# A mixture-of-experts kernel: seven blocks that hold the last halves of two experts each, with their own weight slots

## The chip, the cores and the metric

The kernel runs on one core of a Trainium2 chip. The metric is the device time in microseconds of one execution, lower is better. The core has five engines that run side by side and wait for each other by semaphores: TensorE (PE; its weight loads are listed as PEld), VectorE (DVE), ScalarE (ACT), GpSimd (POOL) and SyncE (SP), the last used for issuing transfers alone. Transfers run on 16 DMA engines that all queues share.

## What is computed

One layer of a streaming encoder for 4096 prompt rows and 128 sample rows of width 1024, 4224 tokens in all, everything in float32. First a Mamba-2 group and a gated spatial MLP on one input projection, an output projection and a residual; then a mixture of experts, and a last norm. The change is in the mixture:

```
h2 = rms_norm(x, norm2_g)
group  = argmax of 4 group logits;  p_group = its softmax
top 2 of the 8 experts of that group;  weights = p_group * softmax(top 2)
for each (token, expert) pair, sorted by expert, padded to blocks of 128:
    y = (silu(xb @ w_gate[e]) * (xb @ w_up[e])) @ w_down[e]      # 1024 -> 256 -> 1024
out[token] += weight * y
x = x + out;   y_out = rms_norm(x, final_norm_g)
```

There are 32 experts and 2 x 4224 = 8448 pairs. An expert's weights take 3.15 MB: 2.10 MB for gate and up, 1.05 MB for down. For the inputs of the reference the router gives the experts 161 to 445 pairs each.

## The kernel before

Two phases. **Phase 1** walks the 33 tiles of 128 tokens: projections, convolution, scan, output projection, norm and router. Each tile stores its rows x2 (after the residual) and h2 (normed) to HBM, and scatters, for each pair, the token number and its weight into a list per expert (`slot_d`). **Phase 2** is the mixture.

Between them VectorE makes tables (`dve_tables`, L1374 to L1434) from the counts: each expert's count is rounded up to blocks of 128, and for each block of the schedule the tables say where its list stands (`row_i`), in which of the weight slots its expert is, how many weight loads must have landed, and, for each load, which expert and after which block. GpSimd gathers the lists with one indirect transfer (L1480), TensorE turns them (L1597), VectorE writes the index rows: `tok_i` (which row to gather), `first_i` and `last_i`. Each token has two pairs in different blocks. The block that holds the earlier one stores its weighted result to `first_d`; the later one gathers it back, adds it to its own and to x2, takes the norm and stores y. An index that is out of bounds makes the transfer skip that row, so each block does both, each for a part of its rows. In the same stretch VectorE and TensorE update the sample streams' states (L1079, L1080, L553).

Phase 2 runs blocks in pairs (`over_pairs`, L1361): at least 33 pairs, more behind a branch. The blocks go by a software pipeline. For block b the engines do this:

- **TensorE** (`pe_phase2`): gate and up of block b + 1 (L1581, 8 calls that give 16 instructions of 128x512), transposes of block b's gated rows (L1614), transposes of block b + 2's gathered rows (L1566), down of block b (L1621, 4 calls, 8 instructions).
- **ScalarE**: evicts the transposes (L1651, L1640), silu of block b + 1 (L1646), squares of block b - 1 for the norm (L1662), half of the down result times its weight (L1659).
- **VectorE**, in this order: adds the earlier result to block b - 1 (`add_first`, L1684), gate of block b + 1 (L1680), half of the rows of block b + 2 (`rows1`, L1674), the other half of the down result (L1699), the norm of b - 1 (L1688), the residual of b (L1707).
- **GpSimd** (`step`, L1521), all on one queue in this order: gather of the rows of block b + 4 (L1500), the root for b - 1 (L1515), store to `first_d` (L1528), gather of x2 for b + 1 (`residual`, L1529), store of y for b - 1 (L1532), and, after the store to `first_d` has landed, the gather of the earlier results for b + 1 (`earlier`, L1533). Its transfers are listed at the helpers' lines L1488 and L1493.
- **SyncE** (`sp_phase2`) loads the experts in order into four weight slots, two transfers each (L1225, L1228). Three experts are loaded ahead (`load_first`); the k-th load waits until the blocks of expert k - 4 have done their gate matmuls, its down part until they have done theirs.

The tail behind the last block is one addition, square, root, norm and store (L1720 to L1722, L1544 to L1558). SyncE ends the kernel when `all_stored` comes.

Of the kernel before, what the change touches and what calls it, by code (L numbers as in the profile page):

```python
# [21 lines left out]
P = 128  # L22
# [52 lines left out]
NCONST = C_ONES + NE  # L75
# [40 lines left out]
GB = 4  # L116
AHEAD = 4
WSLOTS = 4
SET = 3


def build(nc, x_rows, x_cols, consts_in, cols_in, bcast_in, w_in, w_out, w_out_T_in, ws_in, ws_smp_in, cache_in, st_old_in,
          st_T_in, slot_in, w_exp, final_g, y_out, conv_prompt, ssm_prompt, conv_sample, ssm_sample, gmlp_v_sample):
    ctx = ExitStack()
    with ctx:
# [16 lines left out]
        first_d = nc.dram_tensor("first_rows", [T, D], F32).ap()  # L142
# [21 lines left out]
        ones = cst[:, C_ONES:NCONST]  # L164
# [65 lines left out]
        spare = sb("spare", [P, 4])  # L230
# [5 lines left out]
        row_i = sb("row_i", [P, 1], I32)  # L236
# [43 lines left out]
        const_loaded, cols_loaded, bc_loaded, ws_loaded = (sem(n) for n in ("const_loaded", "cols_loaded", "bc_loaded", "ws_loaded"))  # L280
# [11 lines left out]
        gf_loaded = sem("gf_loaded")  # L292
        dve_step, pool_step = sem("dve_step"), sem("pool_step")

        x2_tiles, h2_tiles, first_tiles = (d.rearrange("(t p) d -> t p d", p=P) for d in (x2_d, h2_d, first_d))
# [32 lines left out]
        m_buf = [take(D), xT_mem[1][:, 0:D]]  # L328
        xr_buf = [xT_mem[0][:, 0:D], g2_b]
# [234 lines left out]
        def pe_phase1(pe):  # L564
# [11 lines left out]
            pe.wait_ge(const_loaded, 16)  # L576
# [505 lines left out]
        def dve_phase1(dve):  # L1082
# [38 lines left out]
            dve.wait_ge(ws_loaded, 16)  # L1121
            dve.wait_ge(const_loaded, 16)
# [120 lines left out]
        def sp_turn(sp, tn):  # L1243
# [17 lines left out]
            if tn.prev:  # L1261
                sp.wait_ge(s["x2_part"], 3 * i)
                sp.dma_start(at_tile(x2_tiles, i - 1), x_res[v][:, :]).then_inc(x2_stored, 16)
                if tn.end:
                    load_first(sp, 2)
                sp.wait_ge(s["h2_ready"], i)
                sp.dma_start(at_tile(h2_tiles, i - 1), h2[:, :]).then_inc(h2_stored, 16)
# [30 lines left out]
        def sp_phase1(sp):  # L1298
# [25 lines left out]
            sp.dma_start(flat(wsT[:, :, :]), ws_in).then_inc(ws_loaded, 16)  # L1324
# [49 lines left out]
        def dve_tables(dve, st):  # L1374


            nb, some, pend, pstart, nth = (eqt[:, :], em[:, :], oh[:, 0, :], oh[:, 1, :], oh[:, 2, :])
            ni = slots32[:, 0:NE]
            col = [rt[:, c:c + 1] for c in range(12)]
            block, ebase, kth, start, place, last = col[0:6]  # L1380
            dve.wait_ge(s["rank_read"], NT)
            st.link(V.tensor_tensor(ni, carry[:, :], to_count, ALU.add))
            st.link(V.tensor_scalar(ni, ni, 7, None, ALU.logical_shift_right))
            st.link(V.tensor_copy(nb, ni))
            st.inc(V.tensor_scalar(some, nb, 1.0, None, ALU.min))
            st.link(V.tensor_tensor_scan(out=pend, data0=ones[:, 0:NE], data1=nb, initial=0.0, op0=ALU.mult, op1=ALU.add))

            cmp = rk[:, :]
            st.link(V.tensor_scalar(cmp, pend, tok0, None, ALU.is_le))
            st.inc(V.tensor_reduce(ebase, cmp, AX.X, ALU.add))  # L1390
            st.inc(V.tensor_tensor(pstart, pend, nb, ALU.subtract))
            st.link(V.memset(some[:, 0:SET], 1.0))
# [3 lines left out]
            oe = lgs[:, 0:NE]  # L1396
            st.link(V.tensor_scalar(oe, iota_e, ebase, None, ALU.is_equal))
            st.link(V.tensor_tensor(oe, oe, pstart, ALU.mult))
            st.link(V.tensor_reduce(start, oe, AX.X, ALU.add))
            st.link(V.tensor_tensor(place, tok0, start, ALU.subtract))  # L1400
            st.link(V.tensor_scalar(place, place, float(T // P), float(NE * T // P), ALU.min, ALU.add))
            V.scalar_tensor_tensor(out=row_i[:, :], in0=ebase, scalar=float(T // P), in1=place, op0=ALU.mult,
                                   op1=ALU.add).then_inc(s["rows_ready"], 1)
            dve_h2(dve, NP, NP % 2)

            st.inc(V.tensor_tensor_scan(out=nth, data0=ones[:, 0:NE], data1=some, initial=0.0, op0=ALU.mult, op1=ALU.add))
# [4 lines left out]
            st.inc(V.tensor_scalar(tcol[:, 1:2], kth, 1.0, None, ALU.add))  # L1411
            st.link(V.tensor_copy(ni[:, 0:1], kth))
            st.link(V.tensor_scalar(ni[:, 0:1], ni[:, 0:1], WSLOTS - 1, None, ALU.bitwise_and))
            st.link(V.tensor_scalar(ni[:, 1:2], ni[:, 0:1], 1, None, ALU.logical_shift_right))
# [437 lines left out]
```

## Time and profile before

| | us |
|---|---|
| median of 3 runs | 2912.54 (2911.41 to 2916.14) |
| the profiled execution | 2912.39 |
| its span | 2910.5 |
| TensorE busy | 2859.1 |
| VectorE busy | 1580.8 |
| ScalarE busy | 806.9 |
| GpSimd busy | 878.5 |

Phase 1 takes the first two thirds of the span, the tables some 25 us from 1951, phase 2 from 1976 to the end. Busy time counts an engine's instructions, not its waits and not what its sequencer does. A row of a timeline is the start, the duration, engine, line, operation, out<-in with shapes, the number of merged instructions, and in brackets the idle time ahead with what ended it. In the list of transfers the last number is the median time from issue to landing.

### The profile page before, as it was taken

To read this page: it belongs to the slowest core of one execution; us is meant where nothing else is said; L and a number is where in the kernel's file an instruction comes from. 1 tells how busy PE (TensorE), PEld (TensorE's weight loads), DVE (VectorE), ACT (ScalarE), POOL (GpSimd) and SP (SyncE) were. 2 spreads that over 40 slices of the span, in tenths; PEclk is the share of its full clock that TensorE was granted. 3 is DMA by queue.
4 is the path that set the end of the run, shared out by engine and by line. 5 is a ranking of instruction groups with operands and counts; after the bars stand their busy time and mean duration, and the time that the engine had idled before them with its cause. 6 is when DMAs were issued, how large, how long until landed. Compare 5 with 4: busy or idle time off the path is not lost.

```text
span 2910.5 us, 38335 instructions
## 1 busy us (share of the span) xinstructions
PE 2859.1 (98%) x12809; PEld 1890.8 (65%) x12809; DVE 1580.8 (54%) x4163; ACT 806.9 (28%) x1517; POOL 878.5 (30%) x1366
## 2 busy tenths in 40 slices
PE   8999999999999999999999999989999999999997
PEld 6677777677767776777777677754444444444443
DVE  5565555655565655565555656564444444444444
ACT  1223322323232323223222323212222222222222
POOL 0121112111211111121112111214566565666665
PEclk9999999999999999999999999989999999999999
DMA  7221221112121212211121112257675667567653
GB/s 312 106 79 52 73 80 52 59 66 80 52 71 60 74 51 73 74 58 59 66 80 51 61 64 73 75 220 250 246 261 186 221 202 257 202 220 265 245 169 126
DMA packets 109623, 369.01 MB, mean 127 GB/s; under 512 B 39497, under 2 KB 41426, under 8 KB 99442
## 3 DMA queue, kind: packets, MB, share of 16 engines
q1 hardware_dynamic: 48946, 252.91, 23.9%
q0 software_dynamic: 60480, 113.57, 11.8%
q8 instruction: 112, 1.84, 0.2%
q14 instruction: 85, 0.70, 0.1%
HBM read 325.09 MB, written 140.33 MB: 160 GB/s over the span
## 4 chain that ended last, share of the span: by engine, by line
PE 96%; DVE 2%; DMA 1%; issue 0%; POOL 0%; SPq 0%; ACT 0%; POOLq 0%; DVEq 0%; ACTq 0%
PE PB L368 23%; PE PB L1581 19%; PE PB L379 16%; PE PB L463 12%; PE SS L1621 9%; PE YB L463 4%; PE TB L1566 2%; PE YB L417 2%; PE TB L357 1%; DMA arena<-in_w_in 1%; PE SS L426 1%; PE TB L440 1%; PE SS L430 1%; PE TB L404 1%; PE YB L1614 1%; PE MB L408 1%
## 5 line engine op out<-in xcount | busy, mean ns | idle before, releaser
L368 PE MATMUL PB<-arena,hT 128*128 128x512 f32 (+2 forms) x2112 | 726.2, 497 | 1.2 <-DVE arena L1108 0.9
L368 PEld LDWEIGHTS PB<-arena,hT 128*128 128x128 f32 x2112 | 398.2, 191 | 269.4 <-issue 222.0
L1581 PE MATMUL PB<-arena,hT 128*128 x1296 | 569.3, 592 | 0.0
L379 PE MATMUL PB<-hT,arena 128*128 128x128 f32 x4224 | 487.8, 277 | 4.3 <-DVE arena L1096 4.3
L379 PEld LDWEIGHTS PB<-hT,arena 128*128 128x128 f32 x4224 | 482.3, 193 | 8.2 <-issue 4.6
L1581 PEld LDWEIGHTS PB<-arena,hT 128*128 128x128 f32 x1296 | 246.1, 190 | 309.7 <-issue 309.7
L1133 POOL TENSOR_SCALAR rs<-sq 128x2 f32<-128x2 f32 (+1 forms) x66 | 14.1, 214 | 1299.5 <-ACT h L732 960.8
L463 PE MATMUL PB<-arena,tT 128*128 128x274 f32 (+1 forms) x1056 | 358.7, 494 | 0.7 <-ACT tT L636 0.7
L1621 PE MATMUL SS<-arena,xdt 128*128 x640 | 287.9, 592 | 0.0
L463 PEld LDWEIGHTS PB<-arena,tT 128*128 128x128 f32 x1056 | 196.0, 190 | 141.3 <-issue 121.1
L795 DVE SCALAR_TENSOR_TENSOR xc<-xT,cols,xc 128x128 f32<-128x128 f32 x792 | 216.8, 346 | 3.5
L1621 PEld LDWEIGHTS SS<-arena,xdt 128*128 128x128 f32 x640 | 115.4, 190 | 114.8 <-issue 114.8
L1651 ACT ACTIVATE xdt<-YB 128x256 f32<-128x256 f32 x80 | 30.9, 386 | 512.2 <-PE YB L1614 512.2
L1680 DVE TENSOR_TENSOR gv<-ycat,PB 128x256 f32<-128x256 f32 x81 | 34.0, 420 | 209.6 <-ACT ycat L1646 209.6
L732 ACT ACTIVATE h<-x_res 128x1024 f32<-128x1024 f32 x33 | 34.9, 1057 | 386.2 <-DVE x_res L888 386.2
L592 ACT ACTIVATE xT<-PB 128x512 f32<-128x512 f32 x64 | 38.3, 599 | 338.8 <-PE PB L379 338.8
L463 PE MATMUL YB<-arena,tT 128*128 128x274 f32 x528 | 127.6, 394 | 0.0
L793 DVE TENSOR_SCALAR xc<-xT,cols 128x128 f32<-128x128 f32 x264 | 70.8, 342 | 94.2 <-ACT xT L592 88.1
L463 PEld LDWEIGHTS YB<-arena,tT 128*128 128x128 f32 x528 | 99.9, 189 | 22.1
L1688 DVE SCALAR_TENSOR_TENSOR arena<-arena,rs 128x1024 f32<-128x1024 f32 x80 | 102.2, 1277 | 20.7 <-POOL rs L1519 20.6
L1493 POOL DMA_INDIRECT out_y<-arena,bc x80 | 88.9, 1111 | 24.7 <-issue 22.9
L967 DVE TENSOR_TENSOR hT<-hT,TB 128x1024 f32<-128x1024 f32 x33 | 40.3, 1221 | 97.2 <-PE TB L388 97.2
(273 smaller groups left out, 3598.0 us busy)
## 6 DMA issues: line engine op xcount, KB each, us to landing
arena<-in_w_expert SPq DMA_DIRECT2D x32, 2048.0 KB, 8.8
arena<-in_w_expert SPq DMA_DIRECT2D x32, 1024.0 KB, 6.4
h_rows<-h SPq DMA_DIRECT2D x34, 512.0 KB, 2.7
x_in<-in_x_rows SPq DMA_DIRECT2D x33, 512.0 KB, 4.6
hT<-in_x_cols SPq DMA_DIRECT2D x33, 512.0 KB, 3.7
x_res<-in_x_rows SPq DMA_DIRECT2D x33, 512.0 KB, 5.1
dec<-running_sums SPq DMA_DIRECT2D x33, 512.0 KB, 3.6
first_rows<-bc SPq DMA_DIRECT2D x33, 512.0 KB, 4.0
```

Source lines behind the costliest of these rows:

```text
L368: mm = nc.tensor.matmul(out, hT[u][:, k, :], w_group(name)[:, k, :], start=k == 0, stop=k == KD - 1)
L379: mm = nc.tensor.matmul(PB[b][:, c * P:(c + 1) * P], w_block(name, c)[:, k, :], hT[u][:, k, :], start=k == 0, stop=k == KD - 1)
L417: mm = nc.tensor.matmul(bank[:, c], dec[:, h, :], xdt[:, c], start=True, stop=True)
L463: mm = nc.tensor.matmul(out_p[b], tT[:, k, :], w_out_sb[b][:, k, :], start=k == 0, stop=k == KD - 1)
L793: ins = V.tensor_scalar(dst, src, tap[:, w, c:c + 1], cols[:, R_CBIAS + c:R_CBIAS + c + 1], ALU.mult, ALU.add)
L795: ins = V.scalar_tensor_tensor(out=dst, in0=src, scalar=tap[:, w, c:c + 1], in1=dst, op0=ALU.mult, op1=ALU.add)
L967: V.tensor_tensor(hT[u][:, :, :], hT[u][:, :, :], TB[0][:, 0:1, :].broadcast_to([P, KD, P]), ALU.mult).then_inc(s["x_scaled"], 1)
L1493: nc.gpsimd.indirect_dma_start(out=dram, in_=src, in_offset=None, bounds_check=last, oob_is_err=False, out_offset=bass.IndirectOffsetOnAxi ...
L1566: mm = nc.tensor.transpose(TB[k][:, c, :], g_buf[b % GB][:, (4 * k + c) * P:(4 * k + c + 1) * P], ident)
L1581: mm = nc.tensor.matmul(PB[u][:, :], hT[u][:, k, :], arena[:, bass.ds(slot + k * 2 * DE, 2 * DE)], start=k == 0, stop=k == KD - 1)
L1621: mm = nc.tensor.matmul(SS[:, n, :], hTb[:, k, :], arena[:, bass.ds(slot + KD * 2 * DE + k * D + n * 512, 512)], start=k == 0, stop=k == 1)
L1688: V.scalar_tensor_tensor(out=f_buf[u], in0=f_buf[u], scalar=rs[:, u:u + 1], in1=gf_b, op0=ALU.mult, op1=ALU.mult).then_inc(s["fin_out"], 1)
```

## The change

Counts are now taken in units of 64 rows. An expert whose number of units is odd leaves its last unit out of its own blocks, for the first fourteen such experts. Seven **mixed blocks** stand at fixed places in the schedule, 8, 16, ... 56. The rows 0 to 63 of such a block are the last unit of one expert, rows 64 to 127 that of another. For them:

- Matmuls are issued in halves: for each of the 8 + 4 calls two, with 64 stationary columns each, that write partitions 0 to 63 and 64 to 127 and use the weights of two slots of their own.
- Slots 2 and 3 of the arena belong to the mixed blocks; the ring for whole experts has two slots in place of four, so two experts are loaded ahead, and each load waits for the expert before last. TensorE now waits for the gate part and for the down part of a load one by one.
- The mixed weights, two whole experts, are issued by ScalarE (`load_mixed`), at the end of block 2 and of each mixed block but the last.
- A mixed block doesn't finish any row: all its results go to `first_d`, now twice as long, x2 plus its result goes to a buffer in HBM (`part_d`, issued by ScalarE), and the norm, the addition of the earlier result and their counterparts are replaced by clears of one column. Behind the last block the parts are loaded back (SyncE), the other result of each row is gathered (seven gathers), added, squared, rooted, normed and stored by two stores for each mixed block, since the index lists for y are split in two; the second seven wait until the first seven have landed.
- GpSimd's store to `first_d` of every block waits for the gather of the same block's earlier results.
- The tables get the columns for this, and the lists are gathered by two transfers, one for each half.

```diff
-WSLOTS = 4
-SET = 3
+RING = 2
+SET = RING
...
+NMIX = 7
+MIXED = {8 + 8 * j: j for j in range(NMIX)}
...
 def pe_gate_up(pe, b, weights=None):
+    if b in MIXED:
+        pe.wait_ge(mix_loaded, 32 * (MIXED[b] + 1))
...
     for k in range(KD):
+        if b in MIXED:
+            for r, w in two_halves:
+                mm = nc.tensor.matmul(PB[u][r, :], hT[u][:, k, r], w[:, k * 2 * DE:(k + 1) * 2 * DE], start=k == 0, stop=k == KD - 1)
+        else:
             mm = nc.tensor.matmul(PB[u][:, :], hT[u][:, k, :], arena[:, bass.ds(slot + k * 2 * DE, 2 * DE)], ...)
...
+two_halves = ((slice(0, P // 2), SLOT[2]), (slice(P // 2, P), SLOT[3]))
...
+def pe_down_mixed(pe, n):
+    at = KD * 2 * DE + n * 512
+    for k in range(2):
+        for r, w in two_halves:
+            mm = nc.tensor.matmul(SS[r, n, :], hTb[:, k, r], w[:, at + k * D:at + k * D + 512], start=k == 0, stop=k == 1)
...
 # GpSimd, step(b)
     for k in range(2):
         pool.wait_ge(s[f"dn_out{k}"], b + 1)
-    rows_to(first_d[:, :], y_buf[b % GB], first_i, b, first_kept)
+    after(pool, first_back[b % 2], 16 * ((b + 1) // 2))
+    rows_to(first_d[:, :], y_buf[b % GB], first_i, b, first_kept, 2 * T - 1)
     residual(b + 1)
...
 # ScalarE, step(b)
     rows0(b + 2)
+    if b - 1 in MIXED:
+        j = MIXED[b - 1]
+        act.wait_ge(s["x2_added"], b)
+        nc.scalar.dma_start(part_d[:, j * D:(j + 1) * D], f_buf[1 - u]).then_inc(x2_stored, 16)
...
+    if b == 2:
+        act.wait_ge(ssm_stored, 32)
+        load_mixed(0)
+    if b in MIXED and MIXED[b] + 1 < NMIX:
+        load_mixed(MIXED[b] + 1)
+def load_mixed(j):
+    for k in range(2):
+        expert = entry(act, TAB_EXPERT, MIX_ROW + 2 * j + k, 0, NE - 1)
+        nc.scalar.dma_start(SLOT[2 + k], of(expert)).then_inc(mix_loaded, 16)
...
 # VectorE, step(b)
-    if b > 0:
+    if b - 1 in MIXED:
+        after(dve, first_back[1 - u], 16 * (b // 2))
+        V.memset(spare[:, 0:1], 0.0).then_inc(s["first_added"], 1)
+    elif b > 0:
         dve.wait_ge(s["x2_added"], b)
         add_first(1 - u, 16 * (b // 2))
...
 # SyncE, k-th load
-    if k >= WSLOTS:
-        before = entry(sp, TAB_PEND, k - WSLOTS, 1, NBLK + 1)
+    before = entry(sp, TAB_PEND, k - RING, 1, NBLK + 1)
     sp.wait_ge(s["gu_full"], before)
     load_gate_up(sp, expert, k % RING)
     sp.wait_ge(s["dn_full"], before)
+    sp.wait_ge(w_loaded, 32 * k + 16)
     load_down(sp, expert, k % RING)
...
 # GpSimd, behind the last block (the last root and store of y stand between)
+    for j in range(NMIX):
+        late_gather(j)
+    for j in range(NMIX):
+        late_root(j)
+    for b, j in MIXED.items():
+        pool.wait_ge(s["h2_ready"], NT + j + 1)
+        rows_to(y_out, late_sum[j], first_i, b, y_stored[0])
+    pool.wait_ge(y_stored[0], 16 * (used + NMIX))
+    for b in MIXED:
+        rows_to(y_out, late_sum[MIXED[b]], last_i, b, y_stored[1])
```

## Rows read from the trace of the kernel before

**Rows 1.** The page: span, and TensorE's busy time, share and instructions.
```profile
span 2910.5 us, 38335 instructions
PE 2859.1 (98%) x12809; PEld 1890.8 (65%) x12809; DVE 1580.8 (54%) x4163; ACT 806.9 (28%) x1517; POOL 878.5 (30%) x1366
```

**Rows 2.** Stretches of phase 2: us, busy us of PE, PEld, DVE, ACT, POOL; clock; DMA share; GB/s.
```profile
2100.00:2300.00 200.00, 200.00 (x602) 98.47 (x601) 94.91 (x107) 51.17 (x107) 123.35 (x124) 1.00 0.63 217
...
2500.00:2700.00 200.00, 200.00 (x601) 98.61 (x600) 92.30 (x105) 51.07 (x107) 121.89 (x122) 1.00 0.66 228
2700.00:2895.00 195.00, 194.73 (x581) 95.48 (x579) 91.37 (x110) 49.12 (x103) 122.73 (x123) 1.00 0.56 188
```

**Rows 3.** Timeline of TensorE, 2400 to 2460: one block, and the same place five later.
```profile
2400.09 0.38 PE L1614 MATMUL YB<-cst,gv 128*128 128x128 f32 x2
2400.31 1.04 PE L1566 MATMUL TB<-cst,xc 128*128 128x128 f32 x8
2401.18 3.60 PE L1621 MATMUL SS<-arena,xdt 128*128 x8
2404.62 7.03 PE L1581 MATMUL PB<-arena,hT 128*128 x16
...
2457.06 0.38 PE L1614 MATMUL YB<-cst,gv 128*128 128x128 f32 x2
```

**Rows 4.** ScalarE's instruction at L1651, one for each block.
```profile
L1651 ACT ACTIVATE xdt<-YB x80: 384/387/388, 1990.2 to 2890.5; 128x256 f32<-128x256 f32 x80
```

**Rows 5.** Timeline of VectorE, 1953 to 1976: tables, and the first copy of rows.
```profile
1953.43 0.19 DVE L1382 TENSOR_TENSOR ycat<-carry,cst 128x32 int32<-128x32 f32 x1
...
1960.74 0.15 DVE L1425 TENSOR_SCALAR tcol<-rt 128x1 f32<-128x1 f32 x1
...
1967.73 0.29 DVE L1445 SCALAR_TENSOR_TENSOR bc<-bc 128x128 f32<-128x128 f32 x1
...
1974.82 0.68 DVE L1674 COPY hT<-TB 128x512 f32<-128x512 f32 x1
```

**Rows 6.** Timeline of GpSimd behind the last matmul.
```profile
2900.61 1.02 POOL L1488 DMA_INDIRECT arena<-first_rows,bc  x1 [0.31 <-issue]
...
2905.55 1.10 POOL L1493 DMA_INDIRECT out_y<-arena,bc  x1 [0.61 <-issue]
2907.93 0.18 POOL L1558 TENSOR_TENSOR spare<-cst 128x1 f32<-128x1 f32 x1 [1.28 <-DMA out_y<-arena,bc]
```

**Rows 7.** Timeline of VectorE and ScalarE behind the last matmul: norm, sum, square.
```profile
2895.43 1.27 DVE L1688 SCALAR_TENSOR_TENSOR arena<-arena,rs 128x1024 f32<-128x1024 f32 x1
2896.63 1.22 DVE L1707 TENSOR_TENSOR arena<-wsT,bc 128x1024 f32<-128x1024 f32 x1
...
2900.63 1.06 ACT L1662 ACTIVATE h<-arena 128x1024 f32<-128x1024 f32 x1 [5.17 <-DVE arena L1684]
2901.59 0.19 ACT L1662 ACTIVATION_READ_ACCUMULATOR h<-arena 128x1 f32 x1
```

**Rows 8.** Transfers issued in 2079 to 2082, size, us to landing.
```profile
arena<-in_w_expert SPq DMA_DIRECT2D x1, 2048.0 KB, 11.9
...
arena<-first_rows,bc POOLq DMA_INDIRECT x1, 12.2
```

**Rows 9.** Timelines of SyncE and GpSimd, 2080 to 2090.
```profile
2081.28 0.33 SPq L1225 DMA_DIRECT2D arena<-in_w_expert  x1
...
2081.47 1.02 POOL L1488 DMA_INDIRECT arena<-first_rows,bc  x1 [0.65 <-issue]
...
2087.29 1.27 POOL L1493 DMA_INDIRECT first_rows<-x_res,bc  x1 [2.59 <-DVE x_res L1699]
```

**Rows 10.** GpSimd's gathers (L1488) in 1990 to 2895: issue to landing.
```profile
DMA to landing us min/median/max: 2.1/5.1/12.2
```

**Rows 11.** Queues in 2082 to 2087: packets, MB, share of the 16 engines.
```profile
q1 hardware_dynamic: 102, 1.67, 93.0%
q0 software_dynamic: 78, 0.13, 7.1%
```

**Rows 12.** Timelines of VectorE and TensorE, 2093 to 2097.
```profile
2093.77 1.23 DVE L1684 TENSOR_TENSOR arena<-arena 128x1024 f32<-128x1024 f32 x1 [4.17 <-DMA arena<-first_rows,bc]
...
2095.24 0.68 DVE L1674 COPY hT<-TB 128x512 f32<-128x512 f32 x1
...
2096.86 3.60 PE L1581 MATMUL PB<-arena,hT 128*128 x8
```

**Rows 13.** The stretch 1951 to 1956, columns as in rows 2.
```profile
1951.00:1956.00 5.00, 2.93 (x6) 1.35 (x6) 4.39 (x28) 0.21 (x1) 2.00 (x2) 0.50 0.96 405
```

More of the change, by code:

```diff
@@ L235, in build @@
         tcol = sb("tcol", [P, 4])
[L236 removed]
+        row_i = sb("row_i", [P, 2], I32)
+        other_i = sb("other_i", [P, NMIX], I32)
         tok_i = lng_b[:, 3 * P:4 * P].bitcast(I32)
@@ L1374, in dve_tables @@
         def dve_tables(dve, st):
-            nb, some, pend, pstart, nth = (eqt[:, :], em[:, :], oh[:, 0, :], oh[:, 1, :], oh[:, 2, :])
+            nb2, some, pend2, pstart2, nth = (eqt[:, :], em[:, :], oh[:, 0, :], oh[:, 1, :], oh[:, 2, :])
             ni = slots32[:, 0:NE]
+            unit_i, unit = ycat[:, NE:3 * NE].bitcast(I32).rearrange("p (a e) -> p a e", a=2), ycat[:, 3 * NE:5 * NE].rearrange("p (a e) -> p a e", a=2)
+            half_run, mixed, nf2, mixrow, mixexp = (ycat[:, (5 + k) * NE:(6 + k) * NE] for k in range(5))
@@ L1386, in dve_tables @@
-            st.link(V.tensor_tensor_scan(out=pend, data0=ones[:, 0:NE], data1=nb, initial=0.0, op0=ALU.mult, op1=ALU.add))
+            st.link(V.tensor_scalar(unit_i[:, 0, :], ni, 6, None, ALU.logical_shift_right))
+            st.link(V.tensor_scalar(unit_i[:, 1, :], unit_i[:, 0, :], 1, 1, ALU.bitwise_and, ALU.bitwise_xor))
+            st.link(V.tensor_copy(unit, unit_i))
+            half = unit[:, 1, :]
+            st.inc(V.tensor_tensor_scan(out=half_run, data0=ones[:, 0:NE], data1=half, initial=0.0, op0=ALU.mult, op1=ALU.add))
@@ L1388, in dve_tables @@
+            st.link(V.tensor_tensor_scan(out=pend2, data0=ones[:, 0:NE], data1=nf2, initial=0.0, op0=ALU.mult, op1=ALU.add))
             cmp = rk[:, :]
-            st.link(V.tensor_scalar(cmp, pend, tok0, None, ALU.is_le))
+            st.inc(V.scalar_tensor_tensor(out=mixrow, in0=mixrow, scalar=-2.0, in1=mixed, op0=ALU.add, op1=ALU.mult))
+            st.link(V.tensor_scalar(cmp, pend2, f2_of, None, ALU.is_le))
             st.inc(V.tensor_reduce(ebase, cmp, AX.X, ALU.add))
-            st.inc(V.tensor_tensor(pstart, pend, nb, ALU.subtract))
@@ L1546, in pool_phase2 @@
             root_of(1, 2 * used)
+            for j in range(2, 4):
+                late_gather(j)
             pool.wait_ge(s["fin_out"], 2 * used)
@@ L1609, in step @@
                 pe_gate_up(pe, b + 1)
-                slot = entry(pe, TAB_SLOT, b, 0, SLOT_AT[2])
+                if b not in MIXED:
+                    slot, loads = pe_weights(pe, b)
                 pe.wait_ge(s["hb_ready"], b + 1)
@@ L1794 @@
         consts[:, c:c + P] = mask
-    consts[:, C_ONES:] = 1.0
+    consts[:, C_ONES:C_F2] = 1.0
+    consts[:, C_F2] = 2 * (lane - np.sum(lane[:, None] > np.array(list(MIXED))[None, :], axis=1))
+    consts[:, C_QROW:C_ODD] = -1.0
+    consts[:, C_ODD + 1] = 1.0
+    for b, j in MIXED.items():
+        consts[b, C_F2] = 4 * T
+        consts[b, C_QROW:C_QEXP] = (j + 1, NMIX + j + 1)
+        consts[b, C_ODD + 1] = 0.0
+        consts[MIX_ROW + 2 * j:MIX_ROW + 2 * j + 2, C_QEXP] = (j + 1, NMIX + j + 1)
+        consts[:, C_MIXF + j] = 2 * (b - j)
     consts[:, C_ROW:C_IG] = stream[:, None] == np.arange(SB)[None, :]
```

189 lines of the change are left out of this document (133 added, 56 removed).

## The prediction

> **What bounds the kernel now.** I read the shares of the page first: TensorE is busy for 98% of the span [rows 1]. Then the busy time by stretches: in the stage of the experts TensorE is busy 200.00 us of every 200, at full clock, while the DMA engines are taken to 56 to 66% [rows 2]. Then TensorE's timeline there. One block is 0.22 us of transposes of the gated rows, 0.87 us of row transposes, 3.44 us of down matmuls and 6.86 us of the next block's gate and up matmuls; the same instruction recurs after five blocks in 56.97 us, so a block costs 11.39 us with no gap [rows 3]. Each is paid in full whether 128 rows or 10 of them are real. Eighty blocks are run [rows 4], so a block saved is 11.39 us, and anything that makes TensorE wait is added in full.
>
> **The profiled execution** took 2912.39 us with a span of 2910.5; the median shown is 2912.54. The sum is made against 2912.4. A difference under 0.2% (5.8 us) can't be told from none.
>
> **Blocks saved.** The routing counts of the reference's inputs, worked out from its own router, give 79 blocks of 128, run as 40 pairs. Twelve experts have a last block that is half empty by units of 64 (their last rows number 16 to 61). The change takes these twelve out of the padded blocks: 67 full blocks remain, and the seven mixed ones are always run, the seventh empty: 74, or 37 pairs. Six blocks go: 6 x 11.39 = **-68.4 us**.
>
> **The mixed block on TensorE.** Its 12 matmul calls become 24, each with 64 stationary columns and the same 512 moving ones. If the two halves of the columns work at the same time the block costs what it costs now; if one after the other, 3.44 + 6.86 = 10.3 us more [rows 3]. No row shows two halves at work, so the bounds are 0 and 10.3 us. I take 1.4 us: one half of a call can't start before the first of its partner's two instructions is through (0.43 us, at the end of three groups), and little is lost between whole and half array: 7 x 1.4 = **+10 us**. I take the low side because the halves share neither columns, accumulators nor weights. The Trainium skill (TensorE: Matmul & The Clock Gate, "Measured speedup vs the span model") has three column tiles giving 2.38 times, 0.79 of the ideal; an estimate by that page for two is 2.7 us a block, 19 us instead of 10. No run here shows it.
>
> **Head.** The tables are made on VectorE between 1953.43 and 1960.9, and what follows is a chain on the same engine until the first rows are copied at 1974.82, after which the first gate matmuls start [rows 5]. The diff adds nine instructions before the row numbers, about six before the table columns and seven behind the index lists. At 0.16 to 0.28 us plus their link [rows 5] these are 2.0 + 1.2 + 1.9 = **+5 us**. Bounds: 1, if the chain has cover, and 8, if the second gather of lists (an issue of 1.3 us) adds to it.
>
> **Tail.** Today the last store is issued at 2905.55 and the span of 2910.5 ends 4.9 us later [rows 1, 6]. New on GpSimd's queue are seven gathers, seven roots and fourteen stores; an indirect DMA takes 1.02 us and 0.31 between two [rows 6]. VectorE gets seven sums of 1.22 us and seven norms of 1.27, ScalarE seven squares of 1.06 and 0.19 [rows 7]. In order: the seven gathers, around the last root and store, are issued by 2913.8; the last lands 5 us later by the median [rows 10], 2918.8; three sums that wait for it end at 2922.5; seven norms at 2931.5; the stores go out one for each norm but no faster than 1.33 us, the last by 2934.2 (the first can't go before the last root, 2924.9); it lands some 3 us later; the second seven take 9.3 us; the last needs the 4 us from its issue to the end that today's needs (2905.55 to 2910.5, with the issue). That is 2950.5: **+40 us**. Bounds 30 and 50: landings between 2.4 and 5 us. Reading the parts back is issued by SyncE while TensorE still works and hides there.
>
> **Stores and stand-ins in the mixed steps** (a store of the parts, clears in place of an addition and a norm) replace equal or dearer work on engines with idle time: 0. The part's store stands on ScalarE's queue behind the 6 MB below and is wanted some 20 us later.
>
> **The loads.** This term decides. Seven times two whole experts, 2 x 3.15 MB, are loaded on a queue of their own just behind a mixed block. What a bulk load does to GpSimd's row transfers is to be seen in one case of before. A 2 MB load was issued at 2081.28 and landed 11.9 us later; a gather of earlier rows, issued 0.2 us behind it, landed after 12.2, where the median of GpSimd's gathers is 5.1 [rows 8 to 10]. Between 2082 and 2087 the load's queue had 93% of the DMA engines, and GpSimd's 7.1% [rows 11]: it stands nearly still. VectorE waited 4.17 us for this gather, and its copy ended at 2095.92, 0.9 us before the next gate matmuls began at 2096.86 [rows 12]. So a 5 us load in that place uses the cover up to 0.9 us. The mixed load moves three times as much: by the rate of those 5 us (1.67 MB), some 19 us.
> On top of it the change lets GpSimd wait, ahead of the store of first rows, until the gather of the same block has landed. In the case above that store was issued at 2087.29 and the gather landed at 2093.7 [rows 8, 9], so it would have gone out 6.4 us later, with the residual gather, the store of y and the next gather queued behind it; VectorE's additions wait for those and TensorE for VectorE. The cover is thinner before the mixed loads even come.
> Per mixed load, then: the store of first rows of the mixed block goes out at about the time of the load and lands with it; the next gather, held until then, lands some 5 to 8 us past its due time. I take 5 us of TensorE idle, and 1.5 more since the granted clock was 0.50, the lower of its two levels, in a stretch in which TensorE was busy for 2.93 of 5.00 us [rows 13]: 7 x 6.5 = **+45 us**. Bounds: 0 (all absorbed) and 90 (the whole load less the cover, 13 us each).
> The ring of two costs nothing of itself: a gate load goes out when the last block of the expert before last has done its gate matmuls, and is wanted two blocks (about 27 us) later, one block (16 us) at three experts that have but one; it lands within 11.9 us at worst [rows 8]. If a mixed load meets it, it is still inside 27.
>
> **Sum:** 2912.4 - 68.4 + 10 + 5 + 40 + 45 = **2944 us**.
>
> **Rivals.**
> *The cover holds* (20%): slower transfers are swallowed by the four row buffers and by GpSimd's idle time. For it: before has loads in every second block and no gap [rows 2]. Against: 0.9 us left in the case above. 2912.4 - 68.4 + 55 = 2899 us: faster. The side is decided by the stall per mixed load: under 1.9 us the change gains, above it loses.
> *The queues take turns* (13%): a transfer of GpSimd is let in between the two expert loads and between these and the ring's. The stall then is the length of one load less the cover, some 3 us each without a fall of the clock: 7 x 3 = 21, 2920 us. The gather above came in right behind one load, which fits this as well as a full stop. The Trainium skill has this as a rule (DMA: Bandwidth & Descriptors, "Queues, rings and completion order"): each DMA engine goes round its queues and drains one packet of descriptors from each. The trace's one case neither bears it out nor speaks against it; by that rule the sum would be 2920 instead of 2944.
> *Halves in turn* (14%): the half-array matmuls do not overlap, and the change doesn't do what it says: 7 x 10.3 in place of 10, 3006 us.
> *The new wait binds everywhere* (16%): also beside the ring's 32 loads each store of first rows goes out late, and TensorE loses about 1 us at each: 30 us more, 2974 us.
> The forecast's own case, 2925 to 2965, has 37%.
>
> **How the numbers follow.** The range goes from 2894 (the first rival with 5 us less of tail) to 2990 (the fourth with its bounds) and leaves out the serial halves and a little below. Faster by over 5.8 us is nearly all of the first rival and a small part of the second: 0.21. Within it lies what is between: 0.09. The rest, 0.70, is slower.
>
> **What would show it.** Right: 74 ScalarE copies at the line with 80 now; gate matmuls of a mixed block in about 7.5 us; gaps of TensorE of 3 to 10 us one to three blocks behind each mixed block, ended by a VectorE copy or gate that waited for rows; GpSimd waiting for landings, not for VectorE; a tail of some 55 us behind the last down matmul against 15.8 now. Wrong: no gaps (2899), mixed blocks of 21 us (3006), or a wait for weights in the ring, which I price at nothing.

## The result, and the profile of the changed kernel

The changed kernel took 3091.41 us in the median of 4 runs (3081.86 to 3100.13), beside 2912.16 for the kernel before: 1.0612 times as long, interval 1.0579 to 1.0645. The profiled execution took 3091.76 us. The prediction had the direction and missed the size: 2944 with a range to 2990.

The page of the changed kernel: span, TensorE, the queues (packets, MB, share of 16 engines' span), and the chain of waits by engine.
```profile
span 3089.9 us, 38228 instructions
PE 2845.6 (92%) x12773; PEld 1861.9 (60%) x12773; DVE 1553.6 (50%) x4160; ACT 798.2 (26%) x1495; POOL 841.7 (27%) x1363
q1 hardware_dynamic: 49090, 256.59, 23.0%
q0 software_dynamic: 59200, 134.37, 12.6%
q10 hardware_dynamic: 3024, 47.71, 3.7%
PE 66%; DMA 21%; issue 6%; POOL 4%; DVE 3%; POOLq 0%; SPq 0%; ACT 0%; DVEq 0%; ACTq 0%
```
TensorE is busy for 92% where it was 98% [rows 1], and a fifth of the chain is now transfers. q10 is ScalarE's queue with the mixed loads, q1 SyncE's, q0 GpSimd's. q0 moved 113.57 MB before: 20.8 MB more, although six blocks fewer are run.

The same stretches as in [rows 2], and the two instructions of the mixed block's gate and down (timeline of TensorE).
```profile
2100.00:2300.00 200.00, 169.13 (x504) 78.95 (x503) 69.84 (x84) 40.33 (x84) 90.21 (x98) 0.91 0.77 291
```
```profile
2309.87 7.09 PE L1659 MATMUL PB<-arena,hT 128*64 128x512 f32 x32
...
2321.63 7.03 PE L1661 MATMUL PB<-arena,hT 128*128 x16
...
2329.68 3.65 PE L1672 MATMUL SS<-arena,xdt 128*64 128x512 f32 x16
```
31 us of these 200 are lost, and the granted clock is 0.91. The column halves do overlap: 32 half instructions take 7.09 us where 16 whole ones take 7.03. So the lost time is not in the mixed block's own matmuls.

The waits that carry it (who waited <- for whom: us in all, times, longest).
```profile
DVE arena L1802 <- POOL rs L1562: 281.3, 52, 18.0
POOL first_rows L1536 <- DMA arena<-first_rows,bc: 131.2, 23, 23.0
PE PB L1661 <- DVE hT L1788: 112.5, 20, 14.7
DVE arena L1829 <- DMA out_y<-arena,bc: 82.9, 20, 11.7
POOL xT L1531 <- DMA first_rows<-x_res,bc: 62.2, 9, 14.1
POOL first_rows L1536 <- DMA xT<-first_rows,bc: 46.7, 16, 5.8
PE PB L1661 <- DMA arena<-in_w_expert: 13.9, 1, 13.9
```
TensorE waited 20 times for VectorE's copy of rows (L1788), 112.5 us; VectorE for GpSimd's root, and 20 times for a store of y to land before its residual sum (L1829); and GpSimd for landings: of the gather of earlier rows into one or the other of its two buffers (L1536, the new wait, 39 times in all) and of the store of first rows (L1531, a wait that was there before).

The wait of 13.9 us that the list puts down to weights ended behind VectorE's copy too. That copy ended at 2586.44 and the matmuls began at 2586.80, 0.36 us later (0.39 in the case shown next); the last gate load ahead of it had been issued at 2556.6 and landed 9.3 us after that. Timelines of VectorE and TensorE there:
```profile
2585.76 0.68 DVE L1788 COPY hT<-TB 128x512 f32<-128x512 f32 x1
```
```profile
2586.80 9.96 PE L1661 MATMUL PB<-arena,hT 128*128 x16 [13.91 <-DMA arena<-in_w_expert]
```

One such case beside the mixed block 24, timelines of GpSimd, VectorE and TensorE.
```profile
2330.67 1.02 POOL L1531 DMA_INDIRECT arena<-first_rows,bc  x1 [0.51 <-issue]
...
2344.52 1.07 POOL L1536 DMA_INDIRECT first_rows<-x_res,bc  x1 [10.62 <-DMA arena<-first_rows,bc]
...
2359.30 1.01 POOL L1531 DMA_INDIRECT xT<-first_rows,bc  x1 [11.05 <-DMA first_rows<-x_res,bc]
...
2361.95 0.57 POOL L1562 TENSOR_TENSOR rs<-rs,cst 128x1 f32<-128x1 f32 x1
```
```profile
2362.58 0.06 DVE L1819 MEMSET spare<- 128x1 f32 x1 [16.70 <-POOL rs L1562]
...
2367.54 1.23 DVE L1798 TENSOR_TENSOR arena<-arena,xT 128x1024 f32<-128x1024 f32 x1 [3.59 <-DMA xT<-first_rows,bc]
...
2369.02 0.68 DVE L1788 COPY hT<-TB 128x512 f32<-128x512 f32 x1
```
```profile
2370.09 9.09 PE L1661 MATMUL PB<-arena,hT 128*128 x16 [12.76 <-DVE hT L1788]
```
ScalarE issued the 6 MB at 2334.06. The gather issued at 2330.67 landed near 2344; only then the store of first rows went out; it landed near 2359, and only then the next gather, which landed near 2367.5. Three transfers stand **one behind the other**, the first two beside the bulk, and behind them the root, the clear, the addition and the copy. The gate matmuls then take 9.09 us instead of 7.03. The stretch of their first 4 us (columns as in [rows 2]) has a granted clock of 0.50, the lower of the two levels; from 2374 to 2379 it is 0.99.
```profile
2370.00:2374.00 4.00, 3.91 (x5) 1.85 (x6) 0.36 (x1) 0.53 (x1) 3.04 (x3) 0.50 0.75 257
```
Over all whole blocks this second part of the price can be read from the gate and up matmuls, before and in the change (busy us, then mean ns of one):
```profile
L1581 PE MATMUL PB<-arena,hT 128*128 x1296 | 569.3, 592 | 0.0
```
```profile
L1661 PE MATMUL PB<-arena,hT 128*128 x1088 | 512.1, 626 | 126.6 <-DVE hT L1788 112.5 <-DMA arena<-in_w_expert 13.9 <-issue 0.2
```
Per block of 16 this is 7.03 us and 7.53 us: 34 us over 68 blocks, on top of the 132 us of waits (112.5, 13.9, and 5.7 in front of mixed gates, L1659).

The tail, timeline of GpSimd: first late gather, last root, first and last late store, end.
```profile
3030.23 1.02 POOL L1531 DMA_INDIRECT arena<-first_rows,other_i  x1 [0.57 <-issue]
...
3055.47 1.46 POOL L1597 TENSOR_TENSOR dt_t<-dt_t,cst 128x1 f32<-128x1 f32 x1
...
3057.95 1.93 POOL L1536 DMA_INDIRECT out_y<-arena,bc  x1 [0.17 <-DVE arena L1851]
...
3077.65 0.96 POOL L1536 DMA_INDIRECT out_y<-arena,bc  x1 [0.30 <-issue]
3080.34 0.19 POOL L1631 TENSOR_TENSOR spare<-cst 128x1 f32<-128x1 f32 x1 [1.73 <-DMA out_y<-arena,bc]
```
**The 179.4 us between the spans (2910.5, 3089.9).** Six blocks: -68.4. Head: first gate matmuls at 1979.58 instead of 1976.05, +3.5. Tail, from the last block's first transposes to the end: 76.92 instead of 20.46, +56.5. What the steps between take beyond 11.39 us each: +187.8. Sum 179.4. The question for the runs is the 187.8, of which 132 are waits of TensorE and 36 slower gate matmuls behind them (34, and 2 in the mixed blocks).

### The profile page after: what moved, and what is told of

Its sections match the earlier page's. It is cut to its first block, busy times and chain, and to the rows that moved or that the text cites. A ratio compares the mean times of both kernels' runs of the same rounds, so it can differ in the third digit from the quotient of the medians.

```text
span 3089.9 us, 38228 instructions
## 1 busy us (share of the span) xinstructions
PE 2845.6 (92%) x12773; PEld 1861.9 (60%) x12773; DVE 1553.6 (50%) x4160; ACT 798.2 (26%) x1495; POOL 841.7 (27%) x1363
## 3 DMA queue, kind: packets, MB, share of 16 engines
q10 hardware_dynamic: 3024, 47.71, 3.7%
## 4 chain that ended last, share of the span: by engine, by line
PE 66%; DMA 21%; issue 6%; POOL 4%; DVE 3%; POOLq 0%; SPq 0%; ACT 0%; DVEq 0%; ACTq 0%
PE PB L384 22%; PE PB L395 15%; PE PB L479 11%; DMA arena<-first_rows,bc 6%; DMA first_rows<-x_res,bc 5%; DMA xT<-first_rows,bc 5%; PE YB L479 4%; PE PB L1661 3%; PE YB L433 2%; DMA first_rows<-wsT,bc 2%; DMA first_rows<-tT,bc 1%; DMA out_y<-arena,bc 1%; PE SS L1717 1%; PE TB L373 1%; POOL out_y L1536 1%
## 5 line engine op out<-in xcount | busy, mean ns | idle before, releaser
L1661 PE MATMUL PB<-arena,hT 128*128 x1088 | 512.1, 626 | 126.6 <-DVE hT L1788 112.5
L384 PEld LDWEIGHTS PB<-arena,hT 128*128 128x128 f32 x2112 | 397.4, 191 | 268.9 <-issue 222.0
L1661 PEld LDWEIGHTS PB<-arena,hT 128*128 128x128 f32 x1088 | 216.0, 201 | 416.0 <-issue 415.9
L1717 PE MATMUL SS<-arena,xdt 128*128 x536 | 247.5, 604 | 0.0
L1802 DVE SCALAR_TENSOR_TENSOR arena<-arena,rs 128x1024 f32<-128x1024 f32 x67 | 86.0, 1283 | 281.6 <-POOL rs L1562 281.3
L1717 PEld LDWEIGHTS SS<-arena,xdt 128*128 128x128 f32 x536 | 96.3, 189 | 105.7 <-issue 98.4
L1773 ACT ACTIVATE h<-arena 128x1024 f32<-128x1024 f32 x74 | 78.6, 1062 | 201.3 <-DVE arena L1798 142.8
L1536 POOL DMA_INDIRECT first_rows<-x_res,bc x38 | 58.0, 1527 | 217.6 <-DMA arena<-first_rows,bc 89.7
L1536 POOL DMA_INDIRECT out_y<-arena,bc x88 | 89.5, 1018 | 26.8 <-issue 24.8
```

What stands on the lines that cost most here:

```text
L384: mm = nc.tensor.matmul(out, hT[u][:, k, :], w_group(name)[:, k, :], start=k == 0, stop=k == KD - 1)
L1536: nc.gpsimd.indirect_dma_start(out=dram, in_=src, in_offset=None, bounds_check=last, oob_is_err=False, out_offset=bass.IndirectOffsetOnAxi ...
L1661: mm = nc.tensor.matmul(PB[u][:, :], hT[u][:, k, :], arena[:, bass.ds(slot + k * 2 * DE, 2 * DE)], start=k == 0, stop=k == KD - 1)
L1717: mm = nc.tensor.matmul(SS[:, n, :], hTb[:, k, :], arena[:, bass.ds(slot + KD * 2 * DE + k * D + n * 512, 512)], start=k == 0, stop=k == 1)
L1773: nc.scalar.activation(h2[:, :], f_buf[b % 2], ACT.Square, accum_out=sq[:, b % 2:b % 2 + 1]).then_inc(s["fin_sq"], 1)
L1802: V.scalar_tensor_tensor(out=f_buf[u], in0=f_buf[u], scalar=rs[:, u:u + 1], in1=gf_b, op0=ALU.mult, op1=ALU.mult).then_inc(s["fin_out"], 1)
```

## The experiments

Two suspects stand behind GpSimd's waits: the mixed loads and the new wait. The first runs take away either or both.

**Mixed weights loaded once.** All mixed blocks use the first pair's weights.
```diff
-                if b in MIXED and MIXED[b] + 1 < NMIX:
-                    load_mixed(MIXED[b] + 1)
```


> Leaves out: the mixed blocks 16 to 56 use the weights loaded for the first one, so their rows get other experts' results. Everything else is the changed kernel. Theory L (the loads of 6.3 MB starve GpSimd's row transfers): the excess of the steps over 11.39 us, 188 us in the changed kernel, falls to under 40, time 2940 or less. Theory W (GpSimd's new wait for the gather ahead of the store of first rows makes two transfer times follow each other in every step, so that any load stalls TensorE): gaps remain wherever the ring loads, time 3030 or more. Both together: between, 2960 to 3020.

Measured 3022.81 us, ratio 1.0384 (1.0293 to 1.0474): 69 us less than the change. The two runs lie 22 us apart, so this is rough.

**The new wait taken out.**
```diff
-                after(pool, first_back[b % 2], 16 * ((b + 1) // 2))
```


> The changed kernel without GpSimd's new wait. L: little changes, 3050 or more, gaps still one to three blocks behind the mixed ones. W: the gaps go, 2960 or less. Both: some 3000.

Measured 3023.85, ratio 1.0387 (1.0354 to 1.042): 68 us less. TensorE's waits for L1787 (the copy) fall to 10, one or two behind each mixed load.

**Both.**

> The changed kernel with mixed weights loaded once (later mixed blocks compute with the first one's weights) and without the new wait. Both theories say that TensorE then has no gap behind the start: 2912 - 68 (six blocks) + 4 (head) + 57 (tail) + 15 (0.2 us more in each step) = 2920 us. If it is over 2935, a third cause is at work: the ring of two, or the stand-ins on VectorE that wait for GpSimd's root.

Measured 2938.0, ratio 1.0092 (1.0063 to 1.0122). With neither it is 2938; the wait alone adds 85 us, the loads alone 86, and both 153. Neither theory of one cause holds; there are two, of about the same size. The time is also 18 us above the 2920 expected. In this trace TensorE still waits four times, 12.9 us, once behind the first mixed load, which is still made, and its gate matmuls take 4.7 us more than 68 times 7.03.

**The new wait in the kernel before.**
```diff
+                after(pool, first_back[b % 2], 16 * ((b + 1) // 2))
                 rows_to(first_d[:, :], y_buf[b % GB], first_i, b, first_kept)
```


> The kernel before with the new wait alone. L: the wait is hidden where only the ring loads, within 6 us of 2912. W: it stalls beside the ring's loads, 2935 or more.

Measured 2943.84, ratio 1.0112 (1.0083 to 1.0142), beside 2911.14 in the same round: 33 us, much less than the 85 it costs in the change.

**The loads in six pieces of 1 MB, one behind each of six blocks** (`PIECE_AT = (0, 1, 2, 3, 4, 5)`), with the wait and without it.

> The changed kernel with each pair of mixed experts loaded in six pieces of 1 MB, one behind each of six blocks, in place of two loads of 3 MB at once; the new wait stays. If the length of a load in one piece is what starves GpSimd's transfers (clump theory), this is about the run with loads once: 3010 to 3025. If the added bytes as such do it (42 MB more on the DMA engines), it stays over 3060.

> The same without the new wait. Clump theory: 2930 to 2940, as with the loads taken away (2938), less the 7 us gap that the first mixed load makes at block 5. Bytes theory: 2980 or more.

Measured 3094.07, ratio 1.0623 (1.0592 to 1.0654), and 3026.44, ratio 1.0391 (1.0361 to 1.0421): no gain, and no answer either, since the last pieces came too late. TensorE's waits in the first and the second:
```profile
PE PB L1659 <- DMA arena<-in_w_expert: 67.2, 7, 12.0
PE PB L1661 <- DVE hT L1789: 44.8, 15, 8.0
```
```profile
PE PB L1658 <- DMA arena<-in_w_expert: 64.1, 7, 11.1
PE PB L1660 <- DVE hT L1788: 20.9, 9, 5.4
```
The waits for rows fell from 112.5 to 44.8 and from 76.7 to 20.9 us, and a wait of 9 to 10 us for weights at each mixed gate took their place: a slip of the edit's schedule.

**Pieces early enough** (`PIECE_AT = (0, 1, 2, 3, 4, 4)`, starting two blocks earlier), without the wait.

> The run with six pieces of 1 MB and no new wait, its pieces now issued two steps earlier, since in that run TensorE waited 64 us for pieces that were issued too late. Clump theory (the length of one load starves GpSimd): 2935 to 2950. Bytes theory (the DMA engines are simply short of time): 2980 or more, with the gaps ended by VectorE and not by the load.

Measured 2974.41, ratio 1.0211 (1.0161 to 1.026): 49 us less than with whole loads (3023.85). This is the fastest form of the full change that was found, and it is 2% slower than before.

**The ring of two, alone and with the wait**, on the kernel before.

> The kernel before with the ring of two slots, two experts loaded ahead and TensorE's separate wait for the down part, and nothing else of the change. If the ring costs only the second table entry that TensorE reads for each block (0.17 us in each of 80 steps): 2911 + 14 = 2925. If the ring itself makes waits for weights or new collisions: 2940 or more.

> The ring of two and GpSimd's new wait in the kernel before. The wait alone cost 33 us there, 85 in the changed kernel with the loads taken away. If the ring of two is what makes the difference, this is 2911 + 14 + 85 = 3010; if it is the mixed blocks (all rows stored, stand-ins that wait), it is 2911 + 14 + 33 = 2958.

Measured 2925.03, ratio 1.0044 (1.0024 to 1.0063), and 2964.48, ratio 1.0178 (1.0089 to 1.0267). The ring costs 12.7 us, without any gap. The new wait on top of it costs 39 by the medians, but its two runs lie 22 us apart, so it can't be told from the 33 without the ring. Timeline of TensorE with the ring of two, one block:
```profile
2405.65 0.38 PE L1606 MATMUL YB<-cst,gv 128*128 128x128 f32 x2
2405.86 1.04 PE L1558 MATMUL TB<-cst,xc 128*128 128x128 f32 x8
2406.81 3.70 PE L1614 MATMUL SS<-arena,xdt 128*128 x8
2410.34 7.03 PE L1573 MATMUL PB<-arena,hT 128*128 x16
2417.21 0.38 PE L1606 MATMUL YB<-cst,gv 128*128 128x128 f32 x2
```
A block is 11.56 us instead of 11.39: the down matmuls, which now read the number of loads to wait for from the table besides their slot, and wait for it, take 3.70 us instead of 3.60 [rows 3], and what is in front of them another 0.07. That the reading and the wait are the cause is argued from the edit; no run takes them apart from the smaller ring.

**Earlier rows stored only where they are read.** Ordinary blocks of the change store every row, the later pairs' to the second half of the scratch. Here they skip these (`T - 1` as bound where b isn't mixed); the late gathers read the first half, so the mixed sums are made with other rows. Loads once with the wait; whole loads without the wait; early pieces without the wait.

> The changed kernel with mixed weights loaded once, the new wait on, and the store of an ordinary block to first_d bounded to its first half again (later pairs skipped, as in the kernel before); the sums at the end then skip those rows too. Left out: the other result of tokens whose earlier pair is in a mixed block, and right weights for six mixed blocks. Theory S (the stores of all rows, 21 MB more on GpSimd's queue, make the new wait dear): 3023 falls to about 2938 + 33 = 2970. If the stand-ins of the mixed blocks are what makes it dear: it stays over 3000.

> The changed kernel, mixed loads as they are, without the new wait, and with the store bounded to its half. Left out: the other result of tokens whose earlier pair is in a mixed block. Theory S: the mixed loads cost less too, 2975 to 2990 instead of 3024. If the loads alone do it: 3015 or more.

> All three mended: pieces of 1 MB issued in time, no new wait, half the store (the same sums left out). If these three are the whole of the stall: no gaps, 2912 - 68 + 4 + 54 + 15 = 2917 us. Over 2935 a fourth cause is open.

Measured 2994.19, ratio 1.0279 (1.0217 to 1.034); 3010.37, ratio 1.0334 (1.0304 to 1.0364); 2964.18, ratio 1.0176 (1.0146 to 1.0205). The rows cost 29 us beside the wait (from 3023), 13 beside whole loads (from 3024) and 10 beside pieces (from 2974). The intervals touch those of their partners, so the sizes are rough. Two of the three were expected lower (2970, and 2975 to 2990): the rows are a smaller part than theory S had it. The third was expected at 2917, and over 2935 was to mean a fourth cause. It is at 2964, and the sum is not closed there: TensorE still waits 13 times for VectorE's copy, 28 us, at pieces of 1 MB that cost some 10 us in the run with the ring below. What makes up the rest was not found.

**The same costs one at a time on the kernel before with the ring of two (2925).** The loads here are read by nobody; all computation is unchanged.
```diff
+                for n in range(N_EXTRA):
+                    if b in EXTRA and EXTRA_AT[n] == 0 or b < 56 and EXTRA_AT[n] and b % 8 == EXTRA_AT[n]:
+                        extra_load(n)
```


> The kernel before with the ring of two (measured 2925) and, beside it, seven times two whole experts of 3 MB loaded on ScalarE's queue in steps 2, 8, 16, ... 48 into the two free slots, which nothing reads. No mixed block, no new wait, earlier rows stored as before (only those that are read back). Theory L (the mixed loads alone hold GpSimd's transfers up): what they cost in the change without the wait, 3024 less 2938, is found here again: 86 us, so some 3010 us. Theory A (a good part of that cost came from the extra rows that the change stores, 21 MB on the same queue): clearly less, some 2965 us. TensorE's gaps are 10 to 15 us behind each pair of loads by L, 5 to 6 by A.

> As the run with whole loads beside the ring of two, but each pair of experts comes in six pieces of 1 MB, in steps 0, 1, 2, 3, 4 and 4 of each eight; nothing reads them. If the cost goes by the length of one clump of loads, it falls to about half of what the whole loads cost: 2965 us by theory L, 2945 by theory A. If it goes by the bytes alone, the time is that of the whole loads.

> On the kernel before with the ring of two (2925), seven times 6 MB that nothing reads, in six pieces of 1 MB all issued in one step of each eight. The whole loads cost 76 us (3001), the spread pieces 9 (2934). In the traces a packet of a whole load is 24576 bytes and takes 912 ns, one of a piece 8192 bytes and 309 ns, one of GpSimd's rows 4096 bytes and 159 ns. Theory C (the length of the clump decides, GpSimd stands still until the bulk is through): the pieces at once cost what the whole loads do, some 3000 us. Theory P (the queues of a DMA engine take turns packet by packet, so the size of the bulk's packet decides what is left for GpSimd's rows): they cost far less, some 2940 us. In between: both.

> On the kernel before with the ring of two (2925), seven times two whole loads of 3 MB that nothing reads, three steps apart instead of one behind the other: large packets, half the clump. Theory C: a stall of 11 us behind 6 MB becomes two of the load's length less the cover, some 2 to 3 us each, 2925 + 7 x 5 = 2960 us or less. Theory P (size of the packet alone): about the cost of the whole loads together, 3000 us.

| 7 times 6 MB on ScalarE's queue | us | ratio | cost over 2925 |
|---|---|---|---|
| two whole loads, one behind the other | 3001.52 | 1.0313 (1.0295 to 1.033) | 76 |
| two whole loads, three steps apart | 2996.25 | 1.0305 (1.0266 to 1.0344) | 71 |
| six pieces of 1 MB at once | 2976.81 | 1.0227 (1.0195 to 1.0258) | 52 |
| six pieces over five steps | 2934.18 | 1.009 (1.0059 to 1.0121) | 9 |

The three runs of the last row are 2930, 2934 and 2949, so its cost is 5 to 24 us.

The whole loads cost nearly the 86 us that they cost in the change; extra rows and mixed blocks need not be there (theory L). Theories C and P are each half right: smaller packets in one clump save a third, large packets in two clumps save 5 us, which is inside the spread of the runs, and small packets apart save nearly all. The pieces change the size of the packets and the number of transfers at once; no run takes these two apart.

What the queues show: packets, MB and share of the 16 engines while three of GpSimd's transfers were on their way, in the run with whole loads (2212 to 2219) and in that with six pieces at once (2287 to 2297).
```profile
q10 hardware_dynamic: 125, 2.68, 89.4%
q1 hardware_dynamic: 52, 0.29, 10.1%
q0 software_dynamic: 113, 0.21, 7.7%
```
```profile
q10 hardware_dynamic: 375, 2.81, 68.6%
q0 software_dynamic: 478, 1.05, 26.8%
q1 hardware_dynamic: 28, 0.20, 4.7%
```
The mean packet of q10 is 2.68 MB / 125 = 21 KB in the first and 2.81 / 375 = 7.5 KB in the second, and GpSimd's rows get 0.03 MB a us in the one and 0.105 in the other. The Trainium skill (DMA: Bandwidth & Descriptors, "Queues, rings and completion order") has each DMA engine go round its queues and drain one packet from each in turn; that GpSimd's share is larger beside the smaller packets agrees with it. The median durations in the traces are 912 ns for a packet of 24 KB, 309 for one of 8 KB and 159 for a row of 4 KB. Packet for packet against one bulk queue the rows would get 159 / 1071 = 15% beside the large ones and 159 / 468 = 34% beside the small ones. They got 7.7% and 26.8% beside two bulk queues, and 13.3% over the longer stretch 2204 to 2224 of the first run: the order fits, the shares only roughly.

Where it stalls in the run with whole loads, timelines of GpSimd and TensorE (the two loads were issued at 2201.34).
```profile
2203.32 2.04 POOL L1485 DMA_INDIRECT first_rows<-x_res,bc  x1 [0.23 <-issue]
...
2227.19 1.01 POOL L1480 DMA_INDIRECT xT<-first_rows,bc  x1 [18.17 <-DMA first_rows<-x_res,bc]
```
```profile
2235.70 9.01 PE L1573 MATMUL PB<-arena,hT 128*128 x16 [11.29 <-DVE gv L1689]
```
The store of first rows took some 24 us: the length of the two loads, and then of the ring's next 2 MB, which SyncE issued at 2219.90. The gather behind it could be issued only then. Without the new wait it is the store, not the gather, that eats the cover. A second store lands as late, that of y, issued at 2208.00 (from the chain of waits: start, us):
```profile
2208.00 23.81 DMA out_y<-arena,bc
```
VectorE's residual sum, which waits for it, began at 2231.93, so a faster store of first rows alone would not have closed this gap.

**All rows stored, without and with the wait**, on the same base.

> The kernel before with the ring of two (2925), in which each block stores all of its rows to the scratch of earlier rows, as in the change (rows of the later pairs go to its second half and are never read). It has all 80 blocks, no mixed loads, no new wait. If the rows cost only where GpSimd waits, 2925 to 2930; if the added transfers delay each gather behind them, TensorE shows gaps beside the ring's loads and the time is some 2945.

> As the run in which every row is stored, plus the change's wait: GpSimd holds each store of earlier rows until the gather of the same block has landed. With the ring of two alone the wait made 2964 of 2925. If wait and extra rows add up without touching each other, 2964 plus what the rows alone cost, so 2964 to 2970. If they compound (the store behind the wait is now two to ten times as large and stands between the landing and the next gather), 2985 or more; the change with its loads done once (3023, where none of them costs anything) has then its cause here.

Measured 2929.1, ratio 1.0063 (1.0046 to 1.0079), and 2994.83, ratio 1.0274 (1.0255 to 1.0293). The rows alone cost 4 us, wait and rows together 70, where the wait alone cost 39 (its runs 2954 and 2975, these 2984 to 3012). Of the change's 85 us this is the greater part; the other 15 were not traced. How they compound, timeline of GpSimd in the run with both:
```profile
2162.01 1.01 POOL L1485 DMA_INDIRECT xT<-first_rows,bc  x1 [6.25 <-DMA first_rows<-x_res,bc]
...
2167.00 1.64 POOL L1490 DMA_INDIRECT first_rows<-x_res,bc  x1 [1.76 <-DMA xT<-first_rows,bc]
...
2177.18 1.01 POOL L1485 DMA_INDIRECT arena<-first_rows,bc  x1 [5.90 <-DMA first_rows<-x_res,bc]
...
2182.03 1.77 POOL L1490 DMA_INDIRECT first_rows<-tT,bc  x1 [1.64 <-DMA arena<-first_rows,bc]
```
A gather always waited for the store before it. With the new wait the store waits for the gather too, and the two close a **loop**: gather 4.8 us, store 10.2, gather again. One turn is 15.0 us (2167.00 to 2182.03) and a block 11.56. While loads run beside it, each turn adds what it is longer than the block. By the two pairs of runs (39 and 70 us) the store of every row lengthens its leg of the loop, and the timelines of GpSimd point the same way: where the gather had to wait, it went out 7.5 us behind the store on average with the wait alone (13 times) and 8.9 us with both (27 times).

## Why the prediction was wrong, step by step

**What bounds the kernel** was read rightly: each block's 11.39 us is paid in full, and what stops TensorE is added in full, with the clock on top. Of the signs that were named, the 74 copies, mixed gates in under 7.5 us, gaps ended by VectorE's copy and GpSimd waiting for landings came; the gaps reach 14.7 us where 3 to 10 were named, and the tail behind the last down matmul is 72.1 us, not 55.

**Blocks saved:** right, 74 ScalarE instructions where there were 80, -68.4 us.

**Mixed block:** 10 us forecast, some 2 measured: 0.06 us in the gate, and the down, at 3.65, lies between the whole one's 3.60 of before and 3.70 of after; with a few hundredths around them under 0.3 us a block. The overlap is nearly ideal; the 0.43 us at three groups that the 1.4 us a block were made of did not show. Here the estimate by the Trainium skill's page (TensorE: Matmul & The Clock Gate, "Measured speedup vs the span model"), 19 us, did not hold for two halves with 512 moving columns.

**Head:** 5 forecast, 3.5 measured.

**Tail:** 40 forecast, bounds 30 and 50, 56.5 measured. Two parts of it. The last root was put at 30.2 us behind the last down matmul and ended at 39.1 (3056.9 less 3017.8). The seven gathers were issued by 3043.5, 25.6 us behind it, where 19.1 was taken, and landed late for their sums; and in the last three roots the two instructions took 0.8 to 1.05 and 1.47 us instead of 0.19 and 0.55, beside VectorE's sums and norms. And the last 9.4 us of the span, behind L1631 at 3080.34, hold no instruction of any engine, where before it was 2.4 us [rows 6]; why was not found. It is 9.4 us in the form without wait and repeated loads too.

**Stores and stand-ins at nothing** was the step that hid a cause. It looked at the mixed steps alone. The ordinary steps changed as well: each stores 128 rows to the scratch instead of those that are read back, 20.8 MB more on GpSimd's queue. Alone it is 4 us, so it looks like nothing; behind the new wait it is worth some 30.

**Ring of two at nothing:** right that no weights come late: the one wait that is put down to them, 13.9 us, ended with VectorE's copy. Overlooked was what the down matmuls read and wait for besides: 0.17 us a block, 12.7 us.

**The loads, 45 us**, together with the new wait below, is the step that failed. The measured price of the loads alone is 76 us on the kernel before and 86 in the change, inside the bound of 90 that was kept for them, but far from the value taken. The path was named rightly: the store lands with the load, and the next gather is held until then. Its size was not: the gather was to land 5 to 8 us past its due time and TensorE to idle 5, with 1.5 for the clock, 6.5 in all. By the run with whole loads it is 76 / 7 = 11 us for each pair. The case in [rows 8 to 12] was one gather beside 2 MB; beside 6 MB the store alone took some 24 us. In the change, with the new wait, the gather can be the one that lies under the load as well: its longest landing is 27.3 us.

**The new wait** was seen and its place in the queue told, and then it was treated as a thinner cover in the loads' term, and as a rival of its own at 30 us. It costs 33 us in the kernel before, so that rival's price was right for that kernel; in the change it costs 85. Rivals were set up as alternatives where two of them hold at once: loads and wait together are 153 us, not 45 or 45 + 30. What was missed is that the wait closes a loop of two landings which is longer than a block while loads run, so that nothing is caught up in that time.

**The sum with the measured terms:** 2912.4 - 68.4 + 2 + 3.5 + 56.5 + 12.7 is 2919. With the 18 us of gaps and slower matmuls that the form with neither still has this is 2937, and that form took 2938; 86 for the loads, 85 for the wait, 18 less for what they share: 3091. The last figure is what is left over between the runs, not measured by itself.

Among the rivals, *the queues take turns* had a mechanism that the shares above fit roughly, and a wrong price (three us each, against 11): beside packets of 24 KB the small rows get little. *Halves in turn* and *the cover holds* are excluded by the rows above.

**What would have to be different:** with loads and wait at no cost the change is still at 2938, or at 2919 by the sum without any gap, since head, tail and ring (3.5 + 56.5 + 12.7) eat the 68.4. No form was found that beats the kernel before. A tail with a single store for each mixed block instead of two was not tried.

## What to carry to other kernels

When a change adds a wait between two transfers of one queue, draw the loop that it closes with the waits that are there already, and compare one turn, with the landing times under load, to the step: here it was 15 us against 11.6. A bulk load beside row transfers that others wait for is not priced by its bytes alone: cut into 1 MB pieces over five steps the same seven times 6 MB cost some 9 us instead of 76. Each gap costs more than its length, since the matmuls behind it start at the lower clock: 34 us here on top of 132. And two rivals that don't exclude each other are terms of one sum.

## What the runs showed of the hardware

- Half-array matmuls on the two column halves, each with its own weights, run side by side: 32 of them in 7.09 us, 16 whole ones in 7.03.
- The change, with 6 MB loads on one more queue and the new wait, left the median landing of GpSimd's gathers where it was (5.1 and 5.2 us) and stretched the longest from 12.2 [rows 10] to 27.3 us. GpSimd's gathers (L1531) in the changed kernel, issue to landing:
```profile
DMA to landing us min/median/max: 2.1/5.2/27.3
```
- The second instruction of a root on GpSimd took up to 1.47 us instead of 0.55 beside VectorE's seven norms in the tail.
- With one more table read and one more wait of TensorE in each block (and the smaller ring), a block took 11.56 us instead of 11.39, although no gap of TensorE is seen.
- Matmuls behind a gap of 12.76 us began at a granted clock of 0.50: 9.09 us for 16 that take 7.03.
